# Stick-breaking attention: suffix sums in two float32r passes, the remainder on GpSimd, and the sign bit set on VectorE

## The reference, cut to what matters

```
z      = (q . k) / 8
log1m  = log_sigmoid(-z)            (0 where s >= t)
a[t,s] = exp(log_sigmoid(z) + sum of log1m over the keys between s and t)
out[t] = sum over s of a[t,s] v[s]
```

## Time and profile before

| | us |
|---|---|
| median of 3 runs | 1412.59 |
| lowest, highest | 1410.15, 1412.95 |
| the profiled execution | 1411.0 |
| its span | 1409.2 |
| PE busy | 1351.8 (96%) |
| VectorE busy | 953.2 (68%) |
| ScalarE busy | 673.1 (48%) |
| GpSimd busy | 78.7 (6%) |

### The profile page before, as it was taken

One profiled execution on the slowest core, in us unless ns is written; L12 is line 12 of the kernel. 1 busy time (PEld: TensorE's weight loads), 2 busy tenths in 40 slices (PEclk: granted clock), 3 DMA queues, 4 the chain that ended last, 5 costly groups with the idle time before them and its releaser, 6 DMA issues.

```text
span 1409.2 us, 20047 instructions
## 1 busy us (share of the span) xinstructions
PE 1351.8 (96%) x8392; PEld 1188.6 (84%) x8392; DVE 953.2 (68%) x1197; ACT 673.1 (48%) x882; POOL 78.7 (6%) x148
## 2 busy tenths in 40 slices
PE   6899999999999899999899999999999999999997
PEld 1797789998787789998698878999998987999996
DVE  4698787776697876655784445687777434686774
ACT  1543364444555564444434454654445457654442
POOL 1111011110010200000000010000000000000000
PEclk9999999999999999999999999999999999999999
DMA  9787278887393446555265435355553631454530
GB/s 375 273 345 267 90 278 305 297 295 260 131 364 117 176 164 243 211 199 190 92 235 196 163 122 185 142 211 188 193 185 120 227 132 60 150 210 180 190 138 30
DMA packets 46105, 279.41 MB, mean 198 GB/s; under 512 B 5200, under 2 KB 5200, under 8 KB 18880
## 3 DMA queue, kind: packets, MB, share of 16 engines
q1 hardware_dynamic: 33264, 231.57, 44.9%
q0 software_dynamic: 12752, 46.57, 8.8%
HBM read 277.07 MB, written 1.05 MB: 197 GB/s over the span
## 4 chain that ended last, share of the span: by engine, by line
PE 89%; DVE 5%; ACT 3%; issue 1%; DMA 1%; POOL 0%; SPq 0%; POOLq 0%; ACTq 0%; DVEq 0%
PE ps L1648 35%; PE ps L1774 12%; PE ps L1775 11%; PE ps L1776 11%; PE ps L1710 4%; PE ps L1680 3%; PE ps L2008 1%; PE ps L1741 1%; PE ps L1836 1%; PE ps L1809 1%; DMA ada<-in_ada_w 1%; DVE h_lo L1077 1%; PE ps L2223 1%; DVE x L1109 1%; DVE xn L1107 1%
## 5 line engine op out<-in xcount | busy, mean ns | idle before, releaser
L1009 DVE TENSOR_TENSOR w_lo<-raw,w_hi 128x2048 fp32r<-128x2048 f32 x210 | 479.6, 2290 | 177.1 <-ACT w_hi L606 176.4
L606 ACT ACTIVATE w_hi<-raw 128x2048 fp32r<-128x2048 f32 x210 | 400.4, 1911 | 205.5 <-PE ps L1648 155.8
L1774 PE MATMUL ps<-h_hi,w_hi 128*128 128x256 f32 x1344 | 383.0, 285 | 1.9 <-ACT m_r L783 1.9
L1776 PE MATMUL ps<-h_hi,w_lo 128*128 128x256 f32 x1344 | 381.7, 284 | 0.0
L1775 PE MATMUL ps<-h_lo,w_hi 128*128 128x256 f32 x1344 | 381.7, 284 | 0.0
L1774 PEld LDWEIGHTS ps<-h_hi,w_hi 128*128 128x128 f32 x1344 | 257.5, 192 | 4.1 <-ACT m_r L783 2.3
L1775 PEld LDWEIGHTS ps<-h_lo,w_hi 128*128 128x128 f32 x1344 | 257.4, 191 | 1.8 <-issue 0.2
L1776 PEld LDWEIGHTS ps<-h_hi,w_lo 128*128 128x128 f32 x1344 | 257.4, 192 | 0.0
L1559 DVE SCALAR_TENSOR_TENSOR f_cv<-ps,cols,f_cv 128x254 f32<-128x254 f32 (+1 forms) x176 | 76.7, 477 | 70.9 <-ACT f_cv L918 69.3
L1648 PE MATMUL ps<-w_hi,hid_hi 128*128 128x512 f32 x368 | 114.6, 393 | 0.0
L1648 PE MATMUL ps<-w_hi,hid_lo 128*128 128x512 f32 x368 | 114.4, 392 | 0.0
(11 more groups left out here) (292 smaller groups left out, 1691.0 us busy)
## 6 DMA issues: line engine op xcount, KB each, us to landing
raw<-in_stream SPq DMA_DIRECT2D x210, 1024.0 KB, 4.9
ada<-in_ada_w POOLq DMA_DIRECT2D x80, 512.0 KB, 5.8
ada<-in_ada_w SPq DMA_DIRECT2D x8, 512.0 KB, 12.6
raw<-in_ada_w SPq DMA_DIRECT2D x8, 512.0 KB, 15.8
row<-in_gate_b POOLq DMA_DIRECT2D x3, 512.0 KB, 3.9
x<-in_x SPq DMA_DIRECT2D x1, 1024.0 KB, 9.7
retc<-in_retc POOLq DMA_DIRECT2D x1, 1024.0 KB, 5.1
out<-xn SPq DMA_DIRECT2D x2, 512.0 KB, 2.7
```

The source lines that it names most:

```text
L606: act.activation(w_hi[:, s, :], raw[:, s, :], ACT.Copy).then_inc(hi_done[s], 1)
L1009: dve.tensor_tensor(w_lo[:, s, :], raw[:, s, :], w_hi[:, s, :].bitcast(f32), ALU.subtract)\
L1774: pe.matmul(out, wh, h_hi[:, kt, :], start=kt == 0, stop=False)
L1776: last = pe.matmul(out, wl, h_hi[:, kt, :], start=False, stop=kt == KT - 1)
```

## The change

Five things change, all in the stick-breaking part.

1. The triangle and the all-minus-one matrix are copied once into `maskr` as float32r, beside the identity and the mask (a ScalarE copy of 128x384 at the start of the program).
2. The suffix sums are made with float32r matmuls. The softplus is split into a high part `s_high` (a VectorE copy to float32r) and the remainder `s_rest` (a subtraction on GpSimd), and both go through the matrices.
3. The absolute value on ScalarE is gone: VectorE reads the scores as integers and sets the sign bit, which gives -|z|, and ScalarE takes the exponential of that.
4. The column blocks of a bank are put in another order (old/old, new/new, old/new), so that one 256-wide float32r matmul adds the mask to both diagonal blocks.
5. The waits follow: `s_log` waits for VectorE (`s_clip`), `s_weights` for GpSimd (`spm`), the subtraction for VectorE (`s_cut`), and `s_soft` for weights(p-2), since `s_high` has two buffers.

```diff
--- before.py
+++ after.py
@@ -156,7 +156,7 @@
         mod = sb("mod", [P, ADA_PARTS * KT])
         gsc = sb("gsc", [P, 4 * KT])
         csil = sb("csil", [P, KT])
-        maskr = sb("maskr", [P, 4 * P], f32r)
+        maskr = sb("maskr", [P, 7 * P], f32r)
         gng = sb("gng", [P, GDV])
         sub = sb("sub", [P, DDV])
         lamc = sb("lamc", [P, 4])
@@ -246,6 +246,8 @@
         s_k = at("s_k", 2048, [KT, T])
         s_v = at("s_v", 4096, [TT, D])
         s_b = at("s_b", 6144, [3, 2, 2, 3 * P])
+        s_rest = at("s_rest", 6144, [3, 2, 2, 3 * P], f32r)
+        s_high = at("s_high", 10752, [2, 2, 3 * P], f32r)
 
         ps = ctx.enter_context(nc.psum_tensor("ps", [P, 8, 512], f32))
         ident = shp[:, S_ID:S_ID + P]
...
@@ -587,8 +591,14 @@
             for h in range(RH_):
                 pool.wait_ge(rsq, 2 * h + 2)
                 inverse_rms(stat[:, 1, 2 * h:2 * h + 2], stat[:, 0, 2 * h:2 * h + 2], 2, RDV).then_inc(rrs, 1)
-            for k in range(5, 9):
-                norm(k)
+            norm(5)
+            norm(6)
+            for p in range(SH_ // 2):
+                pool.wait_ge(s_cut, p + 1)
+                pool.tensor_tensor(s_rest[:, p % 3, 1, :, :], s_b[:, p % 3, 1, :, :], s_high[:, p % 2, :, :].bitcast(f32),
+                                   ALU.subtract).then_inc(spm, 1)
+            norm(7)
+            norm(8)
 
 
         @block.scalar
@@ -716,7 +726,8 @@
             act.wait_ge(lam_sum, 1)
             act.activation(lamc[:, 2:4], lamc[:, 0:2], ACT.Exp).then_inc(lam_exp, 1)
             act.activation(maskr[:, 0:P], ident, ACT.Copy)
-            act.activation(maskr[:, P:4 * P], shp[:, S_CAUS:S_CAUS + 3 * P], ACT.Copy).then_inc(mask_done, 1)
+            act.activation(maskr[:, P:4 * P], shp[:, S_CAUS:S_CAUS + 3 * P], ACT.Copy)
+            act.activation(maskr[:, 4 * P:7 * P], shp[:, S_SBM:S_SBM + 3 * P], ACT.Copy).then_inc(mask_done, 1)
             act.wait_ge(ada_pe, KT)
             for j in range(2):
                 act.activation(srow[0:1, j * 512:(j + 1) * 512], ps[0:1, 2 + j, :], ACT.Copy).then_inc(srow_done, 1)
@@ -950,13 +961,9 @@
 
             def s_log(p):
 
-                act.wait_ge(z_ready, p + 1)
+                act.wait_ge(s_clip, p + 1)
                 ln = s_b[:, p % 3, 0, :, :]
-                if p >= 3:
-                    act.wait_ge(so_mm, p - 2)
-                ac.inc(act.activation(ln, ps[:, s_bank(p):s_bank(p) + 2, 0:3 * P], ACT.Abs))
-                act.wait_ge(act_chain, ac.n)
-                ac.inc(act.activation(ln, ln, ACT.Exp, scale=-1.0))
+                ac.inc(act.activation(ln, ln, ACT.Exp))
                 act.wait_ge(act_chain, ac.n)
                 act.activation(ln, ln, ACT.Ln, bias=shp[:, S_ONE:S_ONE + 1]).then_inc(sln, 1)
 
@@ -1589,23 +1596,37 @@
             for c in range(C_SQ, C_SQ + 10):
                 lo(c + 4)
 
+            def s_min(p):
+
+                dve.wait_ge(z_ready, p + 1)
+                if p >= 3:
+                    dve.wait_ge(so_mm, p - 2)
+                dve.tensor_scalar(s_b[:, p % 3, 0, :, :].bitcast(i32), ps[:, s_bank(p):s_bank(p) + 2, 0:3 * P].bitcast(i32),
+                                  -2 ** 31, None, ALU.bitwise_or).then_inc(s_clip, 1)
+
             def s_soft(p):
 
                 dve.wait_ge(sln, p + 1)
-                if p >= 3:
-                    dve.wait_ge(e_mm, p - 2)
-                dve.scalar_tensor_tensor(s_b[:, p % 3, 1, :, :], ps[:, s_bank(p):s_bank(p) + 2, 0:3 * P], 0.0,
-                                         s_b[:, p % 3, 0, :, :], ALU.max, ALU.add).then_inc(spm, 1)
+                if p >= 2:
+                    dve.wait_ge(e_mm, p - 1)
+                sums = s_b[:, p % 3, 1, :, :]
+                link(dve.scalar_tensor_tensor(sums, ps[:, s_bank(p):s_bank(p) + 2, 0:3 * P], 0.0,
+                                              s_b[:, p % 3, 0, :, :], ALU.max, ALU.add))
+                dve.tensor_copy(s_high[:, p % 2, :, :], sums).then_inc(s_cut, 1)
 
             def s_lo(p):
                 dve.wait_ge(so_hi, p + 1)
                 dve.tensor_tensor(h_lo[:, p, :], ps[:, so_bank(p), 0:T], h_hi[:, p, :].bitcast(f32), ALU.subtract)\
                     .then_inc(so_lo, 1)
 
+            s_min(0)
+            s_min(1)
             s_soft(0)
             for p in range(SH_ // 2):
                 if p + 1 < SH_ // 2:
                     s_soft(p + 1)
+                if p + 2 < SH_ // 2:
+                    s_min(p + 2)
                 if p >= 1:
                     s_lo(p - 1)
             s_lo(SH_ // 2 - 1)
@@ -2197,6 +2218,10 @@
             for i in range(3):
                 h_rows(C_SV + i, i, 4)
 
+            def earlier_key(a):
+
+                return a.rearrange("p (j c) -> p j c", j=3)[:, 0:3:2, :]
+
             def s_scores(p):
 
 
@@ -2204,14 +2229,14 @@
                     pe.wait_ge(sexp, p - 2)
                 half = [(slice(i * SDH, (i + 1) * SDH), s_bank(p) + i) for i in range(2)]
                 for f, b in half:
-                    pe.matmul(ps[:, b, 0:T], s_k[f, p, 0:P], s_q[f, p, :], start=True, stop=True)
+                    pe.matmul(earlier_key(ps[:, b, 0:3 * P]), s_k[f, p, 0:P],
+                              s_q[f, p, :].rearrange("p (j c) -> p j c", j=2), start=True, stop=True)
                 for f, b in half:
-                    pe.matmul(ps[:, b, T:T + P], s_k[f, p, P:T], s_q[f, p, P:T], start=False, stop=True,
+                    pe.matmul(ps[:, b, P:2 * P], s_k[f, p, P:T], s_q[f, p, P:T], start=False, stop=True,
                               skip_group_check=True)
                 for f, b in half:
-                    for first in (0, T):
-                        last = pe.matmul(ps[:, b, first:first + P], maskr[:, 0:P], maskr[:, 3 * P:4 * P],
-                                         start=False, stop=True, skip_group_check=True)
+                    last = pe.matmul(ps[:, b, 0:2 * P], maskr[:, 0:P], maskr[:, 3 * P:5 * P], start=False, stop=True,
+                                     skip_group_check=True)
                 last.then_inc(z_ready, 1)
 
             def s_weights(p):
@@ -2219,11 +2244,12 @@
 
                 pe.wait_ge(spm, p + 1)
                 for i in range(2):
-                    sums, b = s_b[:, p % 3, 1, i, :], s_bank(p) + i
-                    pe.matmul(ps[:, b, 0:3 * P], shp[:, S_NU:S_NU + P], sums, start=False, stop=True,
-                              skip_group_check=True)
-                    last = pe.matmul(ps[:, b, P:2 * P], shp[:, S_NO:S_NO + P], sums[:, 2 * P:3 * P], start=False,
-                                     stop=True, skip_group_check=True)
+                    b = s_bank(p) + i
+                    for sums in (s_high[:, p % 2, i, :], s_rest[:, p % 3, 1, i, :]):
+                        pe.matmul(ps[:, b, 0:3 * P], maskr[:, 5 * P:6 * P], sums, start=False, stop=True,
+                                  skip_group_check=True)
+                        last = pe.matmul(ps[:, b, 2 * P:3 * P], maskr[:, 6 * P:7 * P], sums[:, P:2 * P], start=False,
+                                         stop=True, skip_group_check=True)
                 last.then_inc(e_mm, 1)
 
             def s_output(p):
@@ -2233,9 +2259,10 @@
                     pe.wait_ge(so_lo, p - 1)
                 half = [(slice(i * SDH, (i + 1) * SDH), 2 * p + i, s_b[:, p % 3, 0, i, :]) for i in range(2)]
                 for f, h, a in half:
-                    pe.matmul(ps[f, so_bank(p), 0:T], s_v[:, 0, h * SDH:(h + 1) * SDH], a[:, 0:T], start=True, stop=False)
+                    pe.matmul(ps[f, so_bank(p), 0:T].rearrange("p (j c) -> p j c", j=2),
+                              s_v[:, 0, h * SDH:(h + 1) * SDH], earlier_key(a), start=True, stop=False)
                 for f, h, a in half:
-                    last = pe.matmul(ps[f, so_bank(p), P:T], s_v[:, 1, h * SDH:(h + 1) * SDH], a[:, T:T + P],
+                    last = pe.matmul(ps[f, so_bank(p), P:T], s_v[:, 1, h * SDH:(h + 1) * SDH], a[:, P:2 * P],
                                      start=False, stop=True)
                 last.then_inc(so_mm, 1)
```

More of the change, by code:

```diff
@@ L352, in build @@
         z_ready = sem("z_ready")
+        s_clip = sem("s_clip")
         sln = sem("sln")
+        s_cut = sem("s_cut")
         mask_done = sem("mask_done")
```

## The result

| | before | changed |
|---|---|---|
| median, us | 1412.77 (4 runs) | 1422.93 (4 runs) |
| lowest to highest | 1410.15 to 1413.25 | 1422.01 to 1424.14 |
| profiled execution / its span | 1411.0 / 1409.2 | 1422.4 / 1420.7 |

The ratio is 1.0082, 95% interval 1.0069 to 1.0094. By the two medians the change costs 10.2 us, by the profiled executions 11.4, and by the ratio 11.6. The direction was forecast; 3.6 us and a range up to 1422.0 were too small.

A forecast was written before the change was run, and what follows sets the result against it. PE bounds the pairs with 0.19 us of slack; after the change the two-pair round trip does. 5.77 - 1.47 - 0.69 = +3.6 us, predicted 1416.2 us, range 1411.5 to 1422.

The forecast's parts named there:

- ahead of the loop: PE from 1147.31 to weights(1): three masks and one weights get shorter, the wait there doesn't bind; -1.47 us.
- loop, weights(1) to weights(7): Three round trips of 9.53 us plus 1.24 once, 29.83 us instead of 24.06: +5.77 us.
- behind it, weights(7) to the projection: PE from weights(7) at 1182.86 to the projection at 1186.56: one weights is shorter, -0.69 us.
- What bounds the kernel: Through the pairs PE bounds at about 4.03 us each; the two-pair line through other engines has 0.19 us slack.
- The round trip: Scores through the other engines to weights, covering two pairs: from 8.07 to 9.53 us, becoming the bound instead of PE.
- The subtraction: Remainder on GpSimd, in the round trip: about 1.65 us, +1.76 with two handoffs; bounds 0.68 and 2.6.
- the mask: PE's mask in each pair: two 256-wide matmuls take 0.24 us instead of 0.50, -0.26.
- the extra of the first round: In the first round VectorE's sign bit of pair 3 stands behind softplus and copy of pair 2: +1.24 us once.
- Weights: Eight float32r matmuls on PE per pair: 4 x 0.173 + 4 x 0.124 = 1.19 us, -0.69; bounds 0.96 and 1.41.
- The clock: Rival, chance 0.03: PE's granted clock falls from 2.4 to 1.2 GHz, its work doubles, +15 us, 1428.
- the window from 460 to 470 us: Evidence against the falling clock: PE busy 6.79 of 10 us there, with the granted clock staying 1.00.
- PE's idle time: Through the pairs PE idles some 1.7 us each, with waits of 1 to 2 us before most 384-wide weights matmuls.

The follow-up runs named there:

- PE kept busy (four waits): Changed kernel plus 20 unneeded 256-wide float32r matmuls on PE ahead of each of weights(2), (4), (6) and 12 ahead of weights(7): 1416.3 us, ratio 1.0033.

## Why the prediction was wrong

| us against before | forecast | PE kept busy (four waits) | changed kernel |
|---|---|---|---|
| ahead of the loop, first scores to weights(1) (11.49) | -1.47 | -1.14 | -1.16 |
| loop, weights(1) to weights(7) (24.06) | +5.77 | +6.50 | +10.67 |
| behind it, weights(7) to the projection (3.70) | -0.69 | -0.63 | +1.38 |
| sum | +3.6 | +4.7 | +10.9 |

Each entry is the difference of two starts on PE: for the changed kernel 1158.05 - 1147.72, 1192.78 - 1158.05 and 1197.86 - 1192.78, for the kept busy one 1157.48 - 1147.13, 1188.04 - 1157.48 and 1191.11 - 1188.04.

- **What bounds the kernel** held. PE was the bound with 0.19 us of slack, and the new steps moved the bound to the round trip.
- **The round trip** held in kind and nearly in size. The forecast was 9.53 us, and 9.53 + 1.24 for the first one; at full clock 9.84, 9.89 and 10.83 are measured. The subtraction (1.81 for 1.65) and the mask (0.34 for 0.24), each met three times, add 0.48 + 0.30 us, where the loop is longer by 0.73. That the sum comes so near is in part luck: the extra of the first round is 1.0 and not 1.24, and the extra matmuls' own delay makes up for some of it.
- **Weights** came out at 1.19 as summed, but the split was wrong: 384 wide matmuls start 0.22 us before their 128 wide partner, and that takes 0.06, not 0.124.
- **Ahead of the loop** 0.3 us less was gained, again by the mask.
- **The clock** is the step that failed: the sum of +3.6 us had no term for it. I had it as a rival at 0.03, and set the total with it at +15 by letting all of PE's work run at half, 11.8 us of it by the clock. It came in part: in the loop it costs 10.67 - 6.50 = 4.2 us, behind it 2.0. Against it I had put the window from 460 to 470 us, where PE is busy 6.79 of 10 us at a clock of 1.00. That row could not carry it: a busy share says nothing of how long the idle pieces are, and the longest wait of PE in it is 1.49 us.
- **PE's idle time** was spread wrongly: I had 1.7 us in each pair and looked for waits of 1 to 2 us before most weights. It came in one piece of 3.0 to 3.2 us for every two pairs. Even at full clock, with the extra matmuls counted as idle, there are 3.3 us ahead of weights(2), 1.0 ahead of (3) and 2.4 ahead of (4).

The two effects also feed each other: at half clock, weights, output and scores of the round trip are longer, so the round trip itself grows, by 1.7, 1.6 and 0.9 us in the three rounds.

The range ended at 1422.0 with all step costs at their upper bounds and no clock in it. The right form would have been a cost by waits of +4.6 and, on top, up to PE's 3.3 us for a pair at half clock, for some or all of the rounds.

Why the clock falls in one wait and not in another is open. Among the pairs it fell in or shortly behind waits of 3.18 down to 1.84 us (the shortest with the remainder on VectorE) and not at those of 0.8 us, nor at the one of 1.15 us of before. But the length of the wait alone doesn't decide it, as places outside the pairs show, at which all these kernels do the same work. Behind PE's second wait for data, 5.52 us in the kernel before and 5.31 in the changed one, and behind the wait for VectorE's `xn`, 2.49 and 2.51 us, the windows are, first of the kernel before:

```profile
17.12:21.00 3.88, 3.88 (x5) 0.54 (x6) 1.81 (x5) 0.00 (x0) 0.08 (x1) 0.50 1.03 411
685.29:688.00 2.71, 2.49 (x14) 1.88 (x14) 1.93 (x3) 1.40 (x5) 0.00 (x0) 1.00 0.00 0
```

and then of the changed one:

```profile
17.31:21.00 3.69, 3.69 (x5) 0.53 (x6) 1.81 (x4) 0.00 (x0) 0.10 (x1) 1.00 1.02 409
685.67:688.50 2.83, 2.83 (x12) 2.54 (x13) 1.93 (x3) 1.52 (x5) 0.00 (x0) 0.61 0.00 0
```

Each wait is followed by the half clock in one kernel and by the full clock in the other. So the trace of before had work at half clock behind a long wait, at 17.12, of which the prediction says nothing; and a wait at full clock there would not have shown that the same wait is safe in the next kernel.

## What to carry to other kernels

When work moves off the bounding engine, follow one unit round all engines and back, and compare that round trip with the engine's own work; saved time shows only down to the larger of the two, and here the slack was 0.19 us. If the forecast has TensorE idle for microseconds in one piece, let the range hold both prices for the work behind each such piece, at full and at half clock. The half clock costs only what runs through PE: by the traces, about 1 us with the loop on VectorE and ScalarE, and 4.2 with PE in the loop. A few matmuls that nobody needs, in a wait that is there anyway, tell the two costs apart in one run, and here they were worth 6.6 us (5.5, each against its own before).

## What the runs showed of the hardware

A float32 subtraction of 768 elements with two SBUF inputs and a float32r output takes GpSimd 1.80 to 1.85 us; VectorE does it in 0.96.

The copy on VectorE, 0.56 us otherwise, took 1.20 once: the one time that it started while GpSimd was subtracting. The timelines of VectorE and of GpSimd in the changed kernel:

```profile
1154.65 1.20 DVE L1615 CAST s_high<-s_b 128x768 fp32r<-128x768 f32 x1
```

```profile
1153.58 1.85 POOL L598 TENSOR_TENSOR s_rest<-s_b,s_high 128x768 fp32r<-128x768 f32 x1 [67.19 <-DVE s_high L1615]
1155.93 1.82 POOL L598 TENSOR_TENSOR s_rest<-s_b,s_high 128x768 fp32r<-128x768 f32 x1 [0.50 <-DVE s_high L1615]
```

The first subtraction ends at 1155.43 and the copy at 1155.85, 0.42 later. The Trainium skill ("SBUF — State Buffer", Who interferes with whom) says that the two engines share one pair of SBUF ports, that a VectorE copy between SBUF tiles can need it, and that the later one waits until the first has finished. The trace agrees: 1.20 against 0.56 us. Here it cost nothing, since it fell beside the value projection.
